# Two transformer blocks on one core: three modulation slabs beside each early projection, eight beside the first attention

## What is computed

```python
def _adaln(cond, w, b):
    mod = jax.nn.silu(cond) @ w + b
    return tuple(m[:, None, :] for m in jnp.split(mod, 6, axis=-1))
```

```python
h_lat = _modulate(x, norm_mix_g[layer], sh1, sc1)
h_ctx = _modulate(ctx, norm_mix_g[layer], csh1, csc1)
y_lat, y_ctx = _token_mixer(h_lat, h_ctx, w_in[layer], ...)
x = x + g1 * y_lat
x = x + g2 * _peer(_modulate(x, norm_ffn_g[layer], sh2, sc2), ...)
```

## Time and profile before

| | |
|---|---|
| median of 3 runs | 1656.39 us (1656.16 to 1660.06) |
| profiled execution | 1654.45 us, span 1652.6 us |
| PE busy | 1347.8 us, 82% of the span |
| DVE busy | 780.2 us, 47% |
| ACT busy | 452.7 us, 27% |
| POOL busy | 316.1 us, 19% |
| DMA | 583.53 MB, mean 353 GB/s |

### The profile page before, as it was taken

One profiled execution on the slowest core, in us unless ns is written; L12 is line 12 of the kernel. 1 busy time (PEld: TensorE's weight loads), 2 busy tenths in 40 slices (PEclk: granted clock), 3 DMA queues, 4 the chain that ended last, 5 costly groups with the idle time before them and its releaser, 6 DMA issues.

```text
span 1652.6 us, 19061 instructions
## 1 busy us (share of the span) xinstructions
PE 1347.8 (82%) x7112; PEld 775.1 (47%) x7112; DVE 780.2 (47%) x1887; ACT 452.7 (27%) x1235; POOL 316.1 (19%) x272
## 2 busy tenths in 40 slices
PE   5999999998878888779798887799996665666666
PEld 3467886697435554335344542386841221221122
DVE  2101774427687776788888786627320010010001
ACT  2111214412354433454544443215110000000001
POOL 0000000003344333454454455202000000000000
PEclk7999999999999998899999999999997897898897
DMA  9557236946999999999999999953589999999997
GB/s 396 225 200 300 102 106 262 407 168 282 422 420 420 422 416 413 423 412 413 416 421 421 403 422 421 372 204 120 217 345 427 428 428 427 427 428 427 428 428 303
DMA packets 61713, 583.53 MB, mean 353 GB/s; under 512 B 6848, under 2 KB 7232, under 8 KB 8256
## 3 DMA queue, kind: packets, MB, share of 16 engines
q1 hardware_dynamic: 23040, 302.99, 44.5%
q0 software_dynamic: 36864, 268.45, 39.2%
q10 hardware_dynamic: 1728, 11.03, 1.7%
HBM read 581.39 MB, written 1.05 MB: 352 GB/s over the span
## 4 chain that ended last, share of the span: by engine, by line
PE 41%; DMA 39%; DVE 11%; ACT 4%; issue 3%; POOL 1%; SPq 0%; ACTq 0%; DVEq 0%; PEldq 0%
PE ps L1101 37%; DMA big<-peer_uv,big 16%; DMA slab<-w_stream 13%; DMA big<-w_stream 6%; DVE big L2221 4%; DMA scratch<-w_stream 4%; PE ps L1347 1%; POOL big L674 1%; PE ps L1355 1%; ACT big L927 1%; ACT big L923 1%; DVE big L2232 1%; DVE stat L2097 1%; DVE big L2169 0%; PE ps L1258 0%
## 5 line engine op out<-in xcount | busy, mean ns | idle before, releaser
L1101 PE MATMUL ps<-big 128*128 128x512 f32 (+2 forms) x2054 | 618.2, 570 | 171.5 <-ACT big L927 116.1
L1101 PEld LDWEIGHTS ps<-big 128*128 128x128 f32 (+1 forms) x2054 | 257.0, 178 | 489.2 <-ACT big L927 207.0
L674 POOL DMA_INDIRECT big<-peer_uv,big x256 | 305.1, 1192 | 746.9 <-DVE big L2205 385.8
L2221 DVE CUSTOM_DVE_ANT_0 big<-big 128x1024 f32<-128x1024 f32 x256 | 310.6, 1225 | 122.8 <-DMA big<-peer_uv,big 117.6
L1101 PE MATMUL ps<-xh,slab 128*128 128x128 f32 (+1 forms) x1152 | 172.3, 309 | 1.1 <-ACT xh L724 1.1
L1101 PEld LDWEIGHTS ps<-xh,slab 128*128 128x128 f32 x1152 | 161.0, 197 | 20.7 <-issue 11.7
L1101 PE MATMUL ps<-slab,big 128*32 128x512 f32 x768 | 114.9, 728 | 64.8 <-DMA slab<-w_stream 63.3
L919 ACT ACTIVATE big<-big 128x1 f32<-128x1 f32 x256 | 51.5, 201 | 331.2 <-DVE big L2221 330.9
L2441 DVE TENSOR_TENSOR big<-big,ps 128x512 f32<-128x512 f32 x8 | 5.5, 687 | 228.9 <-PE ps L1101 228.9
L1101 PEld LDWEIGHTS ps<-slab,big 128*32 128x32 f32 x768 | 24.0, 120 | 144.4 <-DMA slab<-w_stream 87.1
L1101 PE MATMUL ps<-slab,xh 128*128 128x256 f32 (+2 forms) x304 | 89.5, 450 | 2.3 <-DMA slab<-w_stream 2.3
(11 more groups left out here) (345 smaller groups left out, 1236.5 us busy)
## 6 DMA issues: line engine op xcount, KB each, us to landing
slab<-w_stream SPq DMA_DIRECT2D x90, 2048.0 KB, 17.4
big<-w_stream SPq DMA_DIRECT2D x35, 2048.0 KB, 32.4
scratch<-w_stream SPq DMA_DIRECT2D x8, 2048.0 KB, 32.2
slab<-w_stream SPq DMA_DIRECT2D x8, 1024.0 KB, 30.5
scratch<-w_stream SPq DMA_DIRECT2D x8, 1024.0 KB, 31.2
big<-w_stream ACTq DMA_DIRECT2D x2, 2048.0 KB, 14.6
big<-peer_uv,big POOLq DMA_INDIRECT x256, 11.3
big<-w_stream SPq DMA_DIRECT2D x2, 1024.0 KB, 6.0
```

Source lines behind the costliest of these rows:

```text
L674: nc.gpsimd.indirect_dma_start(out=uv[b], out_offset=None, in_=peer_uv, in_offset=bass.IndirectOffsetOnAxis(ap=idxu[:, s:s + 1], axis=0)). ...
L1101: ins = nc.tensor.matmul(*a, **kw)
L2221: V.tensor_tensor_reduce(out=u, in0=u, in1=xtok, scale=1.0, scalar=0.0, op0=ALU.mult, op1=ALU.add, accum_out=dots[:, s:s + 1]).then_inc(do ...
```

## The change

Each of the four projections is followed by the rows of three modulation slabs (`ADA_STAGE` = 3), so twelve stand in the projections. Eight are left for the first attention, one for every two heads: the rows at even u, the turn at odd u. The slabs' numbers follow: S_K, S_V, S_GKV and S_Q are 4, 8, 12 and 16 in place of 4, 7, 10 and 13; from `S_BA` on all numbers are as before. The third rows of a projection go to the bank of the first, behind a wait for ScalarE's copy of it; there is a third buffer. The last four of the early slabs are of the second block. VectorE's and ScalarE's steps move with them.

```diff
-S_K, S_V, S_GKV, S_Q = (ADA_FIRST + 3 * i for i in range(4))
-ADA_EARLY = 8
+ADA_STAGE = 3
+S_K, S_V, S_GKV, S_Q = (ADA_FIRST + (1 + ADA_STAGE) * i for i in range(4))
+ADA_EARLY = 4 * ADA_STAGE
 ADA_MIXED = ADA_FIRST + ADA_EARLY
-S_AQ, S_O, S_MG = S_Q + 3, S_Q + 4, S_Q + 5
+S_AQ, S_O, S_MG = (S_Q + 1 + ADA_STAGE + i for i in range(3))
...
-        return S_K + 3 * ((n - ADA_FIRST) // 2) + 1 + (n - ADA_FIRST) % 2
+        return S_K + (1 + ADA_STAGE) * ((n - ADA_FIRST) // ADA_STAGE) + 1 + (n - ADA_FIRST) % ADA_STAGE
...
-                    if blk == 0 and u % 4 != 3:
-                        ada_row(ADA_MIXED + u // 4 * 3 + u % 4, hcT[:, 0:T])
+                    if blk == 0 and u % 2 == 0:
+                        ada_row(ADA_MIXED + u // 2, hcT[:, 0:T])
...
             def early_turns(i):
-                for j in range(2):
-                    ada_turn(ADA_FIRST + 2 * i + j, ada_buf[j], 5 * 512 + 8 * j)
+                for j in range(ADA_STAGE):
+                    ada_turn(ADA_FIRST + ADA_STAGE * i + j, ada_buf[j], 5 * 512 + 8 * j)
 
             def early_rows(i):
-                for j in range(2):
-                    n = ADA_FIRST + 2 * i + j
-                    ada_rows(weights(ada_slab(n)), 0, 6 + j)
+                for j in range(ADA_STAGE):
+                    n = ADA_FIRST + ADA_STAGE * i + j
+                    if j == 2:
+                        pe.wait_ge(adarow_stored, n - 1)
+                    ada_rows(weights(ada_slab(n)), n // ADA_SLABS, 6 + j % 2)
...
                     if blk == 0:
-                        n = ADA_MIXED + u // 4 * 3 + u % 4
-                        if u:
-                            ada_turned(n - 1)
-                        if u % 4 != 3:
+                        n = ADA_MIXED + u // 2
+                        if u % 2:
+                            ada_turn(n, hcT[:, 0:T])
+                        else:
                             ada_rows(weights(ada_slab(n)), 1)
...
-            for n in range(ADA_FIRST, ADA_FIRST + 4):
-                ada(n, 5, 8 * (n % 2))
+            early_ada(0, 2 * ADA_STAGE)
...
-            for n in range(ADA_FIRST + 4, ADA_FIRST + 6):
-                ada(n, 5, 8 * (n % 2))
+            early_ada(2 * ADA_STAGE, 3 * ADA_STAGE)
...
-            for n in range(ADA_FIRST + 6, ADA_MIXED):
-                ada(n, 5, 8 * (n % 2))
+            early_ada(3 * ADA_STAGE, ADA_EARLY)
...
-                    if blk == 0 and u and (u - 1) % 4 != 3:
-                        ada(ADA_MIXED + (u - 1) // 4 * 3 + (u - 1) % 4)
+                    if blk == 0 and u % 2:
+                        ada(ADA_MIXED + u // 2)
```

More of the change, by code:

```diff
@@ L300, in two_block_kernel @@
         uv = [at(big, i * 2 * D, 2 * D) for i in ROW_AT]
-        ada_buf = [at(scratch, i * T, T) for i in range(2)]
+        ada_buf = [at(scratch, i * T, T) for i in range(ADA_STAGE)]
         kT2 = at(scratch, 2048, 2048)
@@ L752, in early_rows @@
             def early_rows(i):
-                for j in range(2):
-                    ada_row(ADA_FIRST + 2 * i + j, ada_buf[j], 6 + j)
+                for j in range(ADA_STAGE):
+                    ada_row(ADA_FIRST + ADA_STAGE * i + j, ada_buf[j], 6 + j % 2)
             for c in (2, 3, 0, 1):
@@ L1365, in apply @@
                                                for c in range(4)], head_filled)
[L1367 to L1372, removed]
                 scores(first)
@@ L1870, in _, with early_ada @@
             bg = rowv("b_gates").rearrange("p (d g h) -> p d g h", d=2, g=2)
-            for n in range(ADA_FIRST, ADA_FIRST + 4):
-                ada(n, 5, 8 * (n % 2))
+            def early_ada(first, end):
+                for n in range(ADA_FIRST + first, ADA_FIRST + end):
+                    ada(n, 5, 8 * ((n - ADA_FIRST) % ADA_STAGE))
+            early_ada(0, 2 * ADA_STAGE)
             dve.wait_ge(late_loaded, 32)
```

## The result

The changed kernel takes 1677.21 us (median of 5 runs, 1676.59 to 1685.39) against 1656.39 us for the kernel before (5 runs). The ratio is 1.0132, with a 95% interval of 1.0109 to 1.0155: slower by 20.8 us. The forecast was 1668, with a range up to 1674. The direction was right, the size was not, and the range was too narrow. The profiled execution took 1677.01 us, 22.6 more than that of before.

A forecast was written before the change was run, and what follows sets the result against it. Projections and first attention were taken as bound by PE, the latter with full DMA engines beside it. 7.2 + 3.4 + 9.2 + 3.4 + 1.0 - 12.3 = +11.9 us on the median 1656.39 gave 1668, range 1662 to 1674.

The forecast's parts named there:

- Rows and turns: Projections: four more slabs' row products cost 7.2 us, and one more turn in each of four stages 3.4 us.
- The waits: Projections: PE waits for the slabs of V, gates and Q, 3.2, 3.0 and 3.0 us, together 9.2 us.
- the landing: Projections: a slab's load lands 7.8 us (V) or 7.6 us (gates, Q) after issue, as in the kernel before.
- The clock: Behind the three slab waits: two falls to half clock, 1.7 us each, 3.4 us; bounds 0 and 5.1.
- rival (d): Projections: slab lands within 5.4 us of release, full clock before the first diagonals; -3.5 us, 1653; chance 0.04.
- The attention: First attention: four fewer slabs and turns give back 9.6 us, three vanished waits for VectorE 2.7; together 12.3 us.
- The rival that the chain of scores would bind: Attention: scores, maximum and exponential bind, so saved PE time returns as idle; half the gain lost, +18, 1674; chance 0.10.
- w_branch_m: End of first attention: its 2 MB load, issued at head 11, comes late; PE waits 1 us, 2 at most.
- The hope that lighter traffic would let it land sooner: End of attention: with fewer slabs loading, w_branch_m might land two microseconds sooner, leaving no wait.
- The rest of the way: Expert rows and second block: same work in both kernels, so a shift at the first attention's end goes through unchanged.

The follow-up runs named there:

- the three kernels without slab waits: Changed kernel with third rows and turns repeated from the second slab (2136.51 us), the same as unused work (1662.41), or third rows made three times (1671.69).
- the one with neither: Changed kernel with the third row product behind K, V and gates made three times and the turns put behind separate tiles: 1666.14 us, ratio 1.0052.
- the turns apart: Changed kernel with a projection's three turns one behind each of the first three tiles of the next, not in a row: 1671.86 us, ratio 1.0098.
- the two built on before: Kernel before with every fourth head's turn behind the applying of the head before, 1653.03 us; the same with each projection's two turns apart, 1655.47 us.

## Why the prediction missed

**Rows and turns.** Right. 7.2 us were predicted for rows and 6.9 came (5.39 - 3.66 = 1.73 us, four times); for turns 3.4 and 3.7.

**The waits.** Right in place, cause and number, too small in size: 3.54 + 3.84 + 3.85 = 11.2 us for 9.2. The step that failed is the landing. I took the 7.8 and 7.6 us of two transfers of before; in the new order the loads took 8.1, 8.4 and 8.4 us. Its form, landing less work, held at three sizes: with 3.7, 5.4 and 8.8 us of work in between the wait is 5.1 to 5.8, 3.2 to 3.9 (over all kernels with that work) and at most 0.3 us. The Trainium skill's fit in DMA: Bandwidth & Descriptors, section "Anatomy of one DMA — SWDGE (gpsimd) path", gave an estimate of 6.8 us; all rows here are above it, by 0.8 to 1.6 us.

**The clock.** This is the step that failed most. I took two falls of three at 1.7 us, 3.4 us, and 5.1 as the upper end. The rows behind the waits lost 1.53 (V), 1.64 (gates) and 2.97 (Q), the last because the low clock held for nearly 7 us, not 3.5. And Q's second group lost 1.69 behind its three turns: 7.8 us in all. Another 0.9 went behind the last three turns, in front of the recurrence's first diagonals, where the clock is at 0.50 from 177 to 183 us; the kernel before has such a stretch there too, but shorter. Two things were missing. The price of a fall is not fixed. And a wait of 3 us is not the only cause: the three kernels without slab waits have low clock behind all nine of their turns in a row in V, the gates and Q, and the one with neither has none. I had priced the third turn at its 0.85 us alone, and I did not ask what a third would do to the clock. The trace of before had a sign of it. Behind its last two turns, the recurrence's small matmuls and a wait of 1.33 us the clock falls (second line with the columns of the earlier trace rows):

```profile
149.25 1.69 PE L1258 MATMUL ps<-big,cst 128*128 128x512 f32 x2 [1.33 <-DVE big L1901]
...
150.00:153.00 3.00, 3.00 (x8) 2.04 (x7) 1.29 (x2) 0.00 (x0) 0.00 (x0) 0.50 1.00 426
```

The prediction has this stretch only as the mean of 0.91 of rival (d).

More of it was there. I had counted falls on three rows. From 60 to 1640 us PE has 32 waits of 2.5 to 4 us there, and 27 of them are followed by the lower level within 4 us; three rows gave two in three. Of the four waits of 3.0 us or more all are, and at three of these the level holds for 6.4 to 6.8 us and not 3.4:

```profile
628.36 3.78 PE L1101 MATMUL ps<-big 128*128 128x512 f32 x4 [3.56 <-ACT big L927]
...
628.50:634.50 6.00, 6.00 (x17) 3.92 (x18) 3.89 (x9) 0.90 (x3) 0.94 (x1) 0.51 1.01 422
```

Read from these four, the forecast would have been three falls of three, and some of them long. The two in three was thus a count too small, and not a property of the waits.

Part of the miss is chance. With the slab waits present, only one of six turns in a row in the middle of V, the gates and Q is followed by low clock, in the changed kernel and the one with w_branch_m earlier together. The latter lost 4.6 us in the same groups, inside the prediction's upper end of 5.1. The traces do not say which of the two amounts is the usual one. The Trainium skill, in TensorE: Matmul & The Clock Gate, section "HAM oscillation — how this bites in real kernels", describes a kernel in which each wait for a DMA is followed by a cold start. The changed kernel agrees three times of three; with the turns apart the wait of 3.65 us in front of Q is followed by full clock, so it is not certain here.

**The attention.** Right, and a little small: 12.3 us predicted, 13.9 measured. Counted from the start of each group on PE to the start of the next, the row products give back 7.5 us, the waits 2.7, the turns 2.7 and the applying 1.0. The first two are as predicted. The turns give 0.5 more than predicted: ahead of transposes a turn takes mostly 0.36 us, ahead of rows it took up to 0.54. The products with the values, the same in number, take 14.9 us for 15.9; the prediction had them unchanged. The rival that the chain of scores would bind is refuted: a pair of heads takes 6.33 us, and PE waits for none of the chain's engines beyond the three short ones that before had too.

**w_branch_m.** 2.06 us for 1, just above the upper bound of 2. The hope that lighter traffic would let it land sooner failed (15.3 us for 14.9).

**The rest of the way.** The prediction let a shift at the end of the attention go through to the end unchanged. In the profiles 19.2 us at the first gather became 22.6 at the end, 2.8 of them behind the wait at 1215.60. The matmuls directly behind that wait took 1.13 us in the profile of before and 1.27 to 2.08 in those of all the others with one round of the experts, the two built on before among them; with one profile each I cannot say whether that of before is the exception. On the medians, 8.3 us at the end for 9.7 at the first gather are within the interval, and gains of 1 to 2 us at the first gather are below what the medians can tell.

**The sum.** 6.9 + 3.7 + 11.2 + 7.8 + 0.9 and 0.3 left over = 30.8 at the first scores; less 13.9, plus 2.1 for w_branch_m and 0.2 left over, 19.2 at the first gather; plus 2.8 at 1215.60 and 0.6 elsewhere, 22.6. Of the 10.7 us between forecast and profile the clock makes 8.1 (7.8 + 0.9 + 2.8 for 3.4), the waits 2.0, w_branch_m 1.1, turns, rows and the three remainders 1.1, and the attention gives 1.6 back. On the medians the miss is 9 us.

That the low clock in the projections belongs to the waits and to the turns in a row is shown, by the kernels that take away one and both. Why it holds 3.4 us at one place and 6.8 at another, why the same wait goes without it in one kernel, why three turns in a row are followed by it nine times of nine without slab waits and once in six with them, and why its sum between 340 and 700 us differs by 10 us between kernels that do the same work there, stays open.

## What to carry to other kernels

Before adding an item to a cycle of loads, divide by the number of buffers: where the cycle comes to equal the ring, the large item always meets its own buffer, prefetch is gone, and the wait is the whole landing less the work between. Price small serial matmuls not by their own time alone but also by the dense work behind them, which may run at half clock (it did at nine places of nine without slab waits); spread them between dense groups. Take the clock's loss as a range and not as a figure: the same projections lost 4.6 us in one execution and 7.8 in another. And take the good part of a change by itself: moving every fourth head's turn behind work that was there anyway gained 4 us (interval 2 to 6), while the change that contained the same gain lost 21.

## What the runs showed of the hardware

Three groups of four 4-column matmuls, 0.93 us apart with 0.35 us of idle time in each, were followed by some 3.4 us of granted clock near 0.5 at all three places in each of the three kernels without slab waits. In the two kernels with the waits and the same turns this was so at one place of six, and an uninterrupted wait of 3.65 us in another kernel was not followed by it. The low level lasted some 3.5 us at some places and nearly 7 at others (147 to 154 us: mean 0.57), and one fall cost 1.4 to 3.1 us. A 2 MB load with its queue empty landed in 7.6 to 8.4 us, and one on ScalarE's queue beside SyncE's stream in 14.9 to 15.3.
